# Seven subtractions of a fused two-layer kernel move from VectorE to GpSimd

## The reference

```python
h = rms_norm_2(x, attn_norm)
z = h @ w_in
splits = np.cumsum([2 * CONV_CH, NSA_WIDTH] + [KV_WIDTH] * 6).tolist()
a_conv, q, kc_r, vc_r, ks, vs, kw, vw, g = jnp.split(z, splits, axis=-1)
conv_out = conv_mixer(a_conv, conv_w, conv_b, conv_ln_g, conv_ln_b)      # depthwise, 31 taps, layer norm, silu
kc = compress(kc_r.reshape(kv_shape), cmp_k_pe, cmp_k_w1, cmp_k_w2)      # and vc
nsa_out = nsa_attention(q, kc, vc, ks, vs, kw, vw, gates)                # 12 query heads, 4 key heads
x = x + jnp.concatenate([conv_out, nsa_out], axis=-1) @ w_out
```

## Time and profile before

| engine | busy us | share of the span |
|---|---|---|
| PE (TensorE matmul) | 733.8 | 96% |
| DVE (VectorE) | 510.4 | 67% |
| ACT (ScalarE) | 369.0 | 48% |
| POOL (GpSimd) | 80.9 | 11% |

### The profile page before, as it was taken

How to read it: one execution, slowest core, us unless ns; L and a number is a source line. 1 busy time by engine, 2 the same in 40 slices (tenths; PEclk the granted TensorE clock), 3 DMA queues, 4 the chain that set the end, 5 groups by cost and what they waited for, 6 DMA issues and landing times.

```text
span 761.5 us, 13543 instructions
## 1 busy us (share of the span) xinstructions
PE 733.8 (96%) x5867; PEld 700.5 (92%) x5867; DVE 510.4 (67%) x613; ACT 369.0 (48%) x508; POOL 80.9 (11%) x76
## 2 busy tenths in 40 slices
PE   5899999999999999999999999999899999999996
PEld 4899999999999999999999999797699999998884
DVE  4998688687575777753447879974575665656361
ACT  3444444443545545544435464586654635354341
POOL 1500111003000000000005000004000321331001
PEclk9799999999999999999999979999999999999998
DMA  8989866876605776775651651333354765664511
GB/s 344 376 282 342 271 211 207 283 284 219 222 15 174 249 238 229 237 257 176 212 174 27 196 167 56 120 103 122 101 167 153 225 204 185 203 205 155 201 48 55
DMA packets 118335, 146.49 MB, mean 192 GB/s; under 512 B 4004, under 2 KB 103556, under 8 KB 118276
## 3 DMA queue, kind: packets, MB, share of 16 engines
q1 hardware_dynamic: 116912, 143.58, 57.2%
q10 hardware_dynamic: 1364, 2.05, 0.8%
HBM read 144.57 MB, written 1.05 MB: 191 GB/s over the span
## 4 chain that ended last, share of the span: by engine, by line
PE 78%; DVE 13%; ACT 5%; issue 2%; DMA 2%; POOLq 0%; SPq 0%; DVEq 0%; ACTq 0%
PE bank L596 55%; PE bank L1090 8%; DVE w_lo L1522 6%; ACT w_hi L1129 3%; DVE mod_acc L1514 3%; PE bank L778 3%; PE bank L917 2%; DMA raw<-in_w_ada 2%; DVE wide L1791 1%; PE bank L881 1%; PE bank L883 1%; PE bank L900 1%; PE bank L656 1%; PE bank L633 1%; PE bank L861 1%
## 5 line engine op out<-in xcount | busy, mean ns | idle before, releaser
L1522 DVE TENSOR_TENSOR w_lo<-raw,w_hi 128x2048 fp32r<-128x2048 f32 x108 | 243.0, 2254 | 118.9 <-ACT w_hi L1129 118.7
L1129 ACT ACTIVATE w_hi<-raw 128x2048 fp32r<-128x2048 f32 x110 | 207.0, 1886 | 220.5 <-PE bank L596 176.9
L596 PE MATMUL bank<-act_hi,w_hi 128*128 128x256 f32 x816 | 227.9, 281 | 0.5 <-ACT act_hi L1286 0.3
L596 PE MATMUL bank<-act_lo,w_hi 128*128 128x256 f32 x816 | 225.7, 278 | 1.4 <-DVE act_lo L1813 0.7
L596 PE MATMUL bank<-act_hi,w_lo 128*128 128x256 f32 x816 | 222.1, 278 | 1.4 <-DVE w_lo L1522 1.4
L596 PEld LDWEIGHTS bank<-act_hi,w_hi 128*128 128x128 f32 x816 | 154.0, 189 | 3.6 <-issue 3.1
L596 PEld LDWEIGHTS bank<-act_lo,w_hi 128*128 128x128 f32 x816 | 153.5, 188 | 2.3 <-DVE act_lo L1813 0.9
L596 PEld LDWEIGHTS bank<-act_hi,w_lo 128*128 128x128 f32 x816 | 151.0, 188 | 1.6 <-DVE w_lo L1522 1.6
L596 PE MATMUL bank<-ffn_hi,w_hi 128*128 128x256 f32 x352 | 97.9, 278 | 0.0
L596 PE MATMUL bank<-ffn_hi,w_lo 128*128 128x256 f32 x352 | 97.3, 276 | 0.6 <-DVE w_lo L1522 0.6
L596 PE MATMUL bank<-ffn_lo,w_hi 128*128 128x256 f32 x352 | 97.2, 276 | 0.0
(11 more groups left out here) (278 smaller groups left out, 1099.2 us busy)
## 6 DMA issues: line engine op xcount, KB each, us to landing
raw<-in_w_in SPq DMA_DIRECT2D x31, 1024.0 KB, 6.6
raw<-in_w_ada SPq DMA_DIRECT2D x24, 1024.0 KB, 6.8
raw<-in_w_gate_up SPq DMA_DIRECT2D x22, 1024.0 KB, 5.1
raw<-in_w_mlp_in SPq DMA_DIRECT2D x16, 1024.0 KB, 5.4
raw<-in_w_mlp_out SPq DMA_DIRECT2D x16, 1024.0 KB, 5.2
raw<-in_w_down SPq DMA_DIRECT2D x10, 1024.0 KB, 5.0
raw<-in_w_out SPq DMA_DIRECT2D x8, 1024.0 KB, 6.7
raw<-in_w_proj_conv SPq DMA_DIRECT2D x2, 1024.0 KB, 5.4
```

Of the source, the lines that this page charges most:

```text
L596: i = e.matmul(dst, lhs, rhs, start=start and k == 0 and (m == 0 or second is not None) and n == 0, stop=stop and k == kt - 1 and n == 2, ...
L1129: e.activation(w_hi[slot][:, 0:kt * n_cols], raw[i % N_RAW][:, 0:kt * n_cols], ACT.Copy).then_inc(hi_split, 1)
L1522: e.tensor_tensor(w_lo[slot][:, 0:kt * n_cols], raw[i % N_RAW][:, 0:kt * n_cols], w_hi[slot][:, 0:kt * n_cols].bitcast(F32), ALU.subtract) ...
```

## The change

The tuple of products whose low parts GpSimd makes grows from two to nine: kw, vs, vw, q1, kc, q2 and vc stand before the two chunks of `w_out`.

```diff
-        POOL_LOW = (OUT2, OUT2 + 1)
+        POOL_LOW = tuple(product_of[name] for name in ("kw", "vs", "vw", "q1", "kc", "q2", "vc")) + (OUT2, OUT2 + 1)
```

## The result

The changed kernel takes 772.95 us (median of 4 runs, 772.24 to 776.39) against 761.66 (760.98 to 763.98) for the one before, measured beside it. The ratio is 1.0152, with a 95% interval of 1.0114 to 1.0190: some 11.6 us slower. The forecast was 772.2.

The account below looks back on a forecast made before the run. The prediction took TensorE as the bound with VectorE right beside it, some 6 us to spare in 69. VectorE's waits for GpSimd accumulate to +10.9 us on the 761.33 median: 772.2 us, range 764.5 to 779.

Parts of the forecast that it names:

- Step 1: At ks and kw: GpSimd's kw subtraction makes VectorE's ks subtraction wait, so TensorE goes on 2.6 us later.
- Step 2: At vs and vw: GpSimd's subtractions hold convolution steps ahead of kw's evacuation, so scores(0) starts +4.0 us in all.
- The walk: The main case, following the engines in time order with whole-instruction waits: +10.9 us, own range 769 to 776, chance 0.52.
- Step 3: At q1: VectorE is held in four convolution steps, softmax(0) comes at 453.8 instead of 448.25, scores(1) still not held.
- Steps 4 and 6: kc's subtraction holds normalise(0), turn(0) +4.2 us; q2's holds the eight convolution steps, TensorE stalls 3.75 us, w1k0 +7.6.
- Step 7: At vc: its subtraction holds the last of eight convolution steps, TensorE stalls 3.2 us, turn(4) comes +10.9 us.
- Step 8: After vc: no moved work is left, TensorE is the bound again, everything behind is shifted by the 10.9 us.
- The load check: VectorE's total load: sheds 15.4 us, stands still about 27, so +12 against the 6 us it had free.
- The rival of the clock: TensorE's clock also falls after idle times of 3 to 4 us, 4.4 us per fall: 774 to 781, chance 0.16.
- The rival of slipping past: VectorE mostly slips past GpSimd in the convolution steps, held some 2.5 us each: 764 to 769, chance 0.20.
- that of no lock: Two-input VectorE instructions don't wait, ks's subtraction is on time: 761.3 to 760.7, chance 0.09 together with no change.

Follow-up runs that it names:

- experiments 5 to 7: Changed kernel with GpSimd's subtractions in eight pieces each: 767.19 us; kernel before plus seven spare GpSimd subtractions: 789.59 us; kernel before plus spare GpSimd memsets: 766.90 us.
- experiment 1: Changed kernel with only kw of the seven low parts on GpSimd: 768.09 us, ratio 1.0086 to the kernel before.
- experiment 2: Changed kernel with the other six low parts on GpSimd and kw left on VectorE: 779.62 us, ratio 1.0251 to the kernel before.
- vs_after_kw: Changed kernel with kw left on VectorE and GpSimd starting vs only when kw is evacuated: 772.42 us, ratio 1.0119 to the kernel before.
- none: Kernel before with the low parts of w_out on VectorE too, so GpSimd makes none: 764.12 us, ratio 0.9998.
- none_ks_early: Kernel before with no low part on GpSimd and ks's subtraction ahead of the reciprocal on VectorE: 762.15 us, ratio 0.9977.
- experiment 4: Changed kernel, all seven on GpSimd, but kw's low part starts only when ks's is done: 774.05 us, ratio 1.0170 to the kernel before.

## Why the prediction was right, and where it was lucky

**The lock.** An instruction of VectorE that has two SBUF inputs stands still for all that is left of GpSimd's subtraction, and the two take turns at whole instructions. That was taken from one row on a narrow tensor_scalar; the rows of after show it for two-input instructions too, and experiments 5 to 7 show that it is GpSimd's reading and the length of its instruction that do it. The Trainium skill (SBUF — State Buffer, "SBUF: two separate sides") gives the rule in that form, and adds that two SBUF inputs clash only with a GpSimd instruction that reads SBUF; the 2.29 us beside memsets agree. The Trainium skill (Perfetto Trace Analysis, "Optimizing Scalar/DVE Operations") warns that moving work between these two engines might not help; that was borne out, as here moving 15.4 us off VectorE cost it 23.

**Step 1** held: 4.79 us for ks's subtraction (4.8 forecast), 3.91 of waiting on TensorE (4.0), and experiment 1 is this step alone.

**Step 2 failed**: scores(0) came +2.6, not +4.0. The walk, less the 1.9 us by which this execution was early, has ks's product end at 431.6; it ended at 433.9, where VectorE's evacuation of it begins, for TensorE ran at half clock in 428 to 430 and for some us around it. So vw was rounded 2 us later than in the walk, and its subtraction began 0.03 us after kw's evacuation had. The four steps ahead of the evacuation met one subtraction instead of two. In experiment 2 the steps ahead of it met three, which is the same race lost. **Step 3** failed the same way and as harmlessly: the maxima of softmax(0) came at 447.44, right after q1's subtraction had begun, and read PSUM; in the walk they were behind it, at 451.9.

**Steps 4 and 6** held by their sizes: the normalise stuck behind kc (4.50 us) and turn(0) at +4.4 (4.2 forecast); the eight steps of 7.55 us, TensorE's stall of 3.15 (3.75) and w1k0 at +7.4 (7.6).

**Step 7** was mis-sized: turn(4) came at +9.3, not +10.9, and the stall of 3.2 us ahead of it isn't there. vc's subtraction ran while VectorE waited twice for TensorE's scores (1.38 and 0.62 us, which in the walk it didn't), so that only 1.23 us of it were a hold. In the stall's place TensorE has w1k0's 1.6 us at half clock; with full clock there (`vs_after_kw`) it stalls 1.72 us, and turn(4) is as late behind w1k0. So vc's term is 1.8 to 1.9 us in both, where the walk had 3.3. **Step 8** then held up to w1v0 (+9.3) and not to the end: the slower clock in 544 to 552 brought it to +10.9. So it is luck that the total agrees with the 10.9 of the walk: a term that was 1.6 us too large met a fall of the clock that the walk didn't have, and that `none` has without any of the work that moved. Up to that fall the mixer stood at +9.3. The load check said about 27 us of standing still and +12 of busy time; it was 22.9 and +7.8, the difference being steps 2, 3 and 7.

**The rival of the clock** was half true. More falls came (0.50 in 428 to 430, 448 to 450 and 486 to 488, 0.79 in 544 to 552), but the early ones replaced that of before, and the one at 486 lay where VectorE was the bound. Only the last is left in the shift at the end, and it doesn't need the change: the idle time ahead of it is in before too, and `none` and `none_ks_early` have the fall with no low part on GpSimd. Whether the change makes such falls more frequent isn't shown. **The rival of slipping past** is refuted by the steps of 6.01 and 7.55 us, and **that of no lock** by the first row of VectorE.

**What was wrong behind the prediction** is the habit of adding such stalls up. By the sum of their terms experiments 2 and 4 were expected at +7 to +9 and came at +19 and +13.0; one (+6.5) and its complement (+19) make 25.5 us, and all seven together 11.6. In the profiles' marks, with less of the clock in them, it is 1.8 and 14.3 against 10.9. What a held instruction costs hangs on what VectorE has next for TensorE at that moment, and a shift of a few us swaps a convolution step that nobody waits for against an evacuation. What stays open is the clock's share: it rests on the mean clocks of repeats without a profile, and no run here held the clock fixed.

## What to carry to other kernels

Before work goes from VectorE to GpSimd, ask what each of its instructions will meet: if both engines read two SBUF tensors, a 4.5 us instruction on GpSimd can take 4.5 us from VectorE to save it 2.2. Move it only to where VectorE is idle or works from PSUM, in pieces as short as VectorE's own instructions, and never ahead of something that TensorE waits for. VectorE's own order is the cheaper place to look: one subtraction moved ahead of a reciprocal took away TensorE's wait for it without any other engine, though the gain in the kernel's time stayed within the noise. And before a profile's total is taken as proof of a sum, see whether a control without the change has the same late steps.

## What the runs showed of the hardware that was not expected

- Two memsets on GpSimd leave VectorE's two-input instructions alone (2.29 us) but do hold its instructions with one input and SBUF at both ends: the tensor_scalar of 128x4 shows 0.59 us instead of 0.16 (1.43 another time), four narrow copies 1.95 instead of 1.13. The SBUF page of the Trainium skill named above has such a split: a GpSimd instruction of any kind clashes with VectorE in a mode that uses both ports, and one that reads SBUF also with two SBUF inputs. That the narrow instructions were in such a mode no run shows.
- GpSimd's subtraction of a tensor from itself took 3.60 us where nothing held it, of two tensors 4.54.
- TensorE's clock was still 1.00 in 422 to 424, within the idle time of 3.91 us. It was 0.62 in 424 to 426 and 0.50 in 428 to 430, when the engine was busy without a gap again (12 matmuls in 2 us): the price of the idle time is paid by the work behind it.
